# Query weights' low part moved to VectorE, both gates in one product, and GpSimd's subtractions cut into pieces

## The reference

```python
h = rms_norm(x, norm1_g) * (1.0 + scale1) + shift1
proj = h @ w_in
x_m, o_pre, i_fw, f_fw, i_bw, f_bw, a_q, a_k, a_v = split(proj)
y = concatenate([mlstm(x_m, o_pre, i_fw, f_fw, ...), dilated_attention(a_q, a_k, a_v, ...)])
x = x + gate1 * (y @ w_out)
x = x + gate2 * expert_choice_ffn(...)          # 16 experts
# second block, two layers on 16 meta tokens + 512
for l in range(2):
    parts = split(h @ w_in_2[l])
    mix = concatenate([retention(...), multiscale_pool(...), forgetting_attention(...)])
    h = layer_norm(ALPHA * h + mix @ w_out_2[l])
    h = layer_norm(ALPHA * h + (silu(h @ w1[l]) * (h @ w3[l])) @ w2[l])
```

## Time and profile before

| | us |
|---|---|
| median of 3 runs | 2998.18 (2996.76 to 3000.45) |
| profiled execution, its own time | 3000.69 |
| its span in the trace | 2998.7 |
| TensorE busy | 2733.4 |
| VectorE busy | 976.3 |
| GpSimd busy | 201.6 |

### The profile page before, as it was taken

One profiled execution on the slowest core, in us unless ns is written; L12 is line 12 of the kernel. 1 busy time (PEld: TensorE's weight loads), 2 busy tenths in 40 slices (PEclk: granted clock), 3 DMA queues, 4 the chain that ended last, 5 costly groups with the idle time before them and its releaser, 6 DMA issues.

```text
span 2998.7 us, 36825 instructions
## 1 busy us (share of the span) xinstructions
PE 2733.4 (91%) x15764; PEld 1949.3 (65%) x15764; DVE 976.3 (33%) x1582; ACT 683.6 (23%) x1169; POOL 201.6 (7%) x149
## 2 busy tenths in 40 slices
PE   6989676999999999999899889999999988999998
PEld 3756455444444444444387848999999775788886
DVE  4545544011111112111353344323324244433323
ACT  3214432001011001100232242222222224222222
POOL 2303010000000000000100500000000050000000
PEclk9999787899999999999999969999999997999998
DMA  7271013799999999999701201223231120132321
GB/s 257 91 259 66 1 31 142 304 420 425 427 427 424 428 428 426 426 426 428 292 30 57 64 1 57 85 82 109 76 97 48 57 64 1 57 108 85 110 77 57
DMA packets 238575, 558.33 MB, mean 186 GB/s; under 512 B 29601, under 2 KB 191779, under 8 KB 213500
## 3 DMA queue, kind: packets, MB, share of 16 engines
q1 hardware_dynamic: 234160, 548.48, 47.7%
q0 software_dynamic: 1552, 5.70, 0.6%
q10 hardware_dynamic: 2748, 2.47, 0.2%
HBM read 552.39 MB, written 4.23 MB: 186 GB/s over the span
## 4 chain that ended last, share of the span: by engine, by line
PE 85%; DVE 9%; ACT 3%; issue 2%; DMA 1%; SPq 1%; DVEq 0%; POOL 0%; PEldq 0%; ACTq 0%; POOLq 0%
PE vpsum L2127 20%; PE vpsum L1991 15%; PE apsum L2127 11%; PE vpsum L2008 8%; PE apsum L1975 4%; PE apsum L2136 3%; PE apsum L2153 2%; PE vpsum L2153 2%; PE vpsum L1773 2%; PE vpsum L1764 1%; PE vpsum L2038 1%; PE vpsum L2268 1%; PE apsum L2038 1%; PE vpsum L1849 1%; PE apsum L2057 1%
## 5 line engine op out<-in xcount | busy, mean ns | idle before, releaser
L1991 PE MATMUL vpsum<-ring,arena 128*64 128x512 f32 x2048 | 449.4, 597 | 0.8 <-ACT arena L964 0.8
L2127 PE MATMUL vpsum<-work_r,wring_r 128*128 128x264 f32 (+1 forms) x2160 | 346.2, 322 | 3.4 <-DVE work_r L1625 3.4
L2127 PEld LDWEIGHTS vpsum<-work_r,wring_r 128*128 128x128 f32 x2160 | 312.2, 189 | 37.6 <-issue 6.0
L2127 PE MATMUL apsum<-stream_r,wring_r 128*128 128x264 f32 (+1 forms) x2208 | 336.2, 312 | 0.0
L1991 PEld LDWEIGHTS vpsum<-ring,arena 128*64 128x64 f32 x2048 | 144.9, 138 | 282.9 <-issue 282.7
L2127 PEld LDWEIGHTS apsum<-stream_r,wring_r 128*128 128x128 f32 x2208 | 308.3, 192 | 22.2 <-issue 1.2
L1529 DVE TENSOR_TENSOR wring_r<-wring,wring_r 128x2048 fp32r<-128x2048 f32 (+2 forms) x97 | 200.3, 2069 | 353.1 <-ACT wring_r L1017 352.9
L2127 PE MATMUL vpsum<-stream_r,wring_r 128*128 128x264 f32 (+1 forms) x1728 | 273.8, 318 | 10.5 <-DVE body L1612 10.5
L1017 ACT ACTIVATE wring_r<-wring 128x2048 fp32r<-128x2048 f32 (+3 forms) x100 | 172.6, 1728 | 469.6 <-DMA wring<-w_ffn 453.0
L2127 PEld LDWEIGHTS vpsum<-stream_r,wring_r 128*128 128x128 f32 x1728 | 247.1, 192 | 31.8 <-DVE body L1612 10.9
L2008 PE MATMUL vpsum<-ring,arena 128*64 128x512 f32 x1024 | 226.8, 595 | 11.0 <-ACT arena L978 11.0
(11 more groups left out here) (428 smaller groups left out, 3145.5 us busy)
## 6 DMA issues: line engine op xcount, KB each, us to landing
ring<-w_gate SPq DMA_DIRECT2D x64, 2048.0 KB, 16.8
ring<-w_up SPq DMA_DIRECT2D x64, 2048.0 KB, 10.1
ring<-w_down SPq DMA_DIRECT2D x64, 2048.0 KB, 13.6
wring<-w_ffn SPq DMA_DIRECT2D x88, 512.0 KB, 4.7
ring<-w_ada SPq DMA_DIRECT2D x12, 2048.0 KB, 13.9
wring<-w_ffn SPq DMA_DIRECT2D x32, 704.0 KB, 4.5
ring<-w_in SPq DMA_DIRECT2D x5, 2048.0 KB, 18.9
wring<-w_in SPq DMA_DIRECT2D x10, 1024.0 KB, 5.4
```

The lines of the kernel that those rows point to most:

```text
L1991: last = pe.matmul(banks[g][CAP * blk:CAP * blk + CAP, :], xin[:, 2 * r + c, :], w[:, at:at + 512], start=r + c == 0, stop=r + c == 4)
L2127: last = pe.matmul(dst, w_[:, c, col:col + P], x_.bitcast(FR), start=c == 0 and i == 0, stop=c == chunks - 1 and i == 2)
```

## The change

- Query weights: the low part is made by VectorE in two halves of 128x2048, after all eight h chunks and before all eight low parts. TensorE waits for the new semaphore `q_low`.
- Gates: `wgate` is 104 columns wide, with the input gates at 0 and the forget gates at 64. One product per chunk fills one bank. The input gates are read with their bias; the forget gates are copied down to partition 0 and get their bias in a second instruction. A stage `gates_even` without contents keeps the count of stages, and the readers of the gates wait for it. The gate readers stand behind the eight low parts.
- GpSimd: the low parts of K_W, V_W, XM_W and O_W are made in four pieces of 1024 columns each, the casts and subtractions of the six units of the second block in four pieces of 512. No wait separates the pieces of one tensor.

```diff
@@
-        wgate = share(768, KC * 80, "p (c k m) -> p c k m", c=KC, k=2)
+        wgate = share(768, KC * GATE_W, "p (c m) -> p c m", c=KC)
@@ def input_low(i):
-                pool.tensor_tensor(ring_r[:, k, :].bitcast(FR), ring[:, k, :], ring_r[:, HIGH_SLOT[i], :], ALU.subtract).then_inc(in_low, 1)
+                for j in range(4):
+                    words = slice(1024 * j, 1024 * j + 1024)
+                    pool.tensor_tensor(ring_r[:, k, words].bitcast(FR), ring[:, k, words], ring_r[:, HIGH_SLOT[i], words], ALU.subtract).then_inc(in_low, 1)
@@
-            for i in (Q_W, K_W, V_W):
+            for i in (K_W, V_W):
                 input_low(i)
@@ for n in range(OP_U + 1, OP_U + 4):
-                    pool.tensor_copy(unit_part(l, n, True).bitcast(FR), unit_part(l, n, False, wring)).then_inc(w_high, 1)
+                    pieces = [slice(512 * j, 512 * j + 512) for j in range(4)]
+                    for piece in pieces:
+                        cut = pool.tensor_copy(unit_part(l, n, True)[:, piece].bitcast(FR), unit_part(l, n, False, wring)[:, piece])
+                    cut.then_inc(w_high, 1)
                     pool.wait_ge(w_high, LU * l + n + 1)
-                    pool.tensor_tensor(unit_part(l, n, False).bitcast(FR), unit_part(l, n, False, wring), unit_part(l, n, True), ALU.subtract).then_inc(w_low, 1)
+                    for piece in pieces:
+                        cut = pool.tensor_tensor(unit_part(l, n, False)[:, piece].bitcast(FR), unit_part(l, n, False, wring)[:, piece], unit_part(l, n, True)[:, piece], ALU.subtract)
+                    cut.then_inc(w_low, 1)
@@ VectorE
                 dve.tensor_scalar(hT[:, c, :], hT[:, c, :], g1s[:, c:c + 1], mod[:, c:c + 1], ALU.mult, ALU.add).then_inc(h_done, 1)
-                if c >= 1:
-                    stream_low(c - 1)
+            at = SLOT_OF[f"in{Q_W}"]
+            dve.wait_ge(in_high, Q_W + 1)
+            for k in range(2):
+                words = slice(2048 * k, 2048 * k + 2048)
+                dve.tensor_tensor(ring_r[:, at, words].bitcast(FR), ring[:, at, words], ring_r[:, HIGH_SLOT[Q_W], words], ALU.subtract).then_inc(q_low, 1)
+            for c in range(KC):
+                stream_low(c)
             dve.wait_ge(gate_in, 16 * 4)
-            for k in range(2):
-                dve.tensor_scalar(gates[0:40, k, :], take("gates", k)[0:40, :], bgate[:, k:k + 1], None, ALU.add).then_inc(v_freed, 1)
-            stream_low(KC - 1)
+            b = take("gates")
+            dve.tensor_scalar(gates[0:40, 0, :], b[0:40, :], bgate[:, 0:1], None, ALU.add).then_inc(gate_out, 1)
+            dve.tensor_copy(gates[0:40, 1, :], b[GATE_AT[1]:GATE_AT[1] + 40, :]).then_inc(gate_out, 1)
+            dve.wait_ge(gate_out, 2)
+            dve.tensor_scalar(gates[0:40, 1, :], gates[0:40, 1, :], bgate[:, 1:2], None, ALU.add).then_inc(v_freed, 1)
+            dve.wait_ge(v_freed, V.count("gates"))
+            take("gates_even")
+            dve.nop().then_inc(v_freed, 1)
@@ TensorE
-                for k in range(2):
-                    last = pe.matmul(banks[k][0:40, :], wgate[:, c, k, :], hT[:, c, :], start=c == 0, stop=c == KC - 1)
-                    if c == KC - 1 and k == 0:
-                        last.then_inc(v_filled, 1)
-                last.then_inc(h_used, 1)
+                pe.matmul(b[0:GATE_W, :], wgate[:, c, :], hT[:, c, :], start=c == 0, stop=c == KC - 1).then_inc(h_used, 1)
```

More of the change, by code:

```diff
@@ L22 @@
 MH, MD = 4, 128
+GATE_AT, GATE_W = (0, 64), 104
 AH, AD = 8, 64
@@ L238, in program @@
         MOD_ROW_AT = {1 + 4 * k: 8 + k for k in range(4)}
-        V = Plan([("xT", KC), ("colsA", 1)] + first_mods() + [("gates", 2), ("aqT", 4), ("akT", 4), ("colsA2", 1), ("colsB", 1), ("bvec", 3),
+        V = Plan([("xT", KC), ("colsA", 1)] + first_mods() + [("gates", 1), ("gates_even", 1), ("aqT", 4), ("akT", 4), ("colsA2", 1), ("colsB", 1), ("bvec", 3),
                   ("xm", MH)] + mod_stages(4, 8) + [("gcol", 2)] + list(attention_stages())
@@ L263, in program @@
         h_high, h_low1, in_high, in_low = sem("h_high"), sem("h_low1"), sem("in_high"), sem("in_low")
-        h_used, qk_scaled, h_normed, wgate_in, wgate_done, h2_scaled = sem("h_used"), sem("qk_scaled"), sem("h_normed"), sem("wgate_in"), sem("wgate_done"), sem("h2_scaled")
+        h_used, qk_scaled, h_normed, wgate_in, wgate_done, gate_out, q_low, h2_scaled = sem("h_used"), sem("qk_scaled"), sem("h_normed"), sem("wgate_in"), sem("wgate_done"), sem("gate_out"), sem("q_low"), sem("h2_scaled")
         wgate_rows = arena[:, 24336:24336 + KC * 16].rearrange("p (c n) -> p c n", c=KC)
@@ L645, in _ @@
                     for d in range(2):
-                        pool.tensor_copy(wgate[:, :, k, 32 * q + 4 * d:32 * q + 4 * d + 4], wgate_rows[:, :, 8 * d + 4 * k:8 * d + 4 * k + 4]).then_inc(wgate_done, 1)
+                        at = GATE_AT[k] + 32 * q + 4 * d
+                        pool.tensor_copy(wgate[:, :, at:at + 4], wgate_rows[:, :, 8 * d + 4 * k:8 * d + 4 * k + 4]).then_inc(wgate_done, 1)
             def input_low(i):
@@ L834, in _ @@
             input_high(K_W)
-            act.wait_ge(v_freed, V.count("gates"))
+            act.wait_ge(v_freed, V.count("gates_even"))
             tmp = gates[0:40, 2, :]
@@ L1777, in inputs @@
             def inputs(i):
-                pe.wait_ge(in_low, i + 1)
+                if i == Q_W:
+                    pe.wait_ge(q_low, 2)
+                else:
+                    pe.wait_ge(in_low, 4 * i)
                 return chunks(ring_r[:, HIGH_SLOT[i], :]), chunks(ring_r[:, SLOT_OF[f"in{i}"], :])
@@ L1788, in _ @@
             pe.wait_ge(wgate_done, 8)
-            banks = [vclaim("gates", k) for k in range(2)]
+            b = vclaim("gates")
             for c in range(KC):
                 pe.wait_ge(h_done, c + 1)
-                for k in range(2):
-                    last = pe.matmul(banks[k][0:40, :], wgate[:, c, k, :], hT[:, c, :], start=c == 0, stop=c == KC - 1)
-                    if c == KC - 1 and k == 0:
-                        last.then_inc(v_filled, 1)
-                last.then_inc(h_used, 1)
+                pe.matmul(b[0:GATE_W, :], wgate[:, c, :], hT[:, c, :], start=c == 0, stop=c == KC - 1).then_inc(h_used, 1)
             pe.wait_ge(h_used, KC)
+            pe.nop().then_inc(v_filled, 1)
+            vclaim("gates_even")
             pe.nop().then_inc(v_filled, 1)
```

## The result

The change makes the kernel faster: 2975.65 us (median of 4 runs, 2974.12 to 2980.6) against 2997.68 of the kernel before on the same chip, a ratio of 0.993 (95% interval 0.991 to 0.994). A second time, with 6 runs: 2976.7 (2969.3 to 2981.6) against 2998.66, 0.992 (0.991 to 0.994). The forecast was 2974.7, range 2966 to 2986. The profiled execution took 2977.05, its span 2975.3, which is 23.4 less than before; the sum said 23.5. The sum came out, but two of its terms did not: place 2 gave less than forecast, the layers more. A second profiled execution of the changed kernel took 2969.43 us, with a span 31.0 us shorter than before, so one pair of traces does not settle the sum.

A forecast was written before the change was run, and what follows sets the result against it. TensorE, busy 91%, was taken to bound the kernel, so gains come only where it waits for VectorE or GpSimd. 8.2 + 7.5 + 7.8 = 23.5 us less than 2998.18 gives 2974.7 us, range 2966 to 2986.

The forecast's parts named there:

- the sum: Whole kernel: gains of 8.2 at the start, 7.5 at the output gate and 7.8 in the layers, together 23.5 us.
- place 2: Output gate stage: shorter GpSimd pieces let VectorE's late chain finish earlier, so TensorE waits less and runs warm; 7.5 us.
- Place 1: Kernel start: query products begin at 56.1 instead of 66.13, less 1.8 us for a cold clock; 8.2 us gained.
- Rival (a): Start and layers: the fast TENSOR_SCALAR does not contend with GpSimd; sum 27.4, time 2970.8 us; chance 0.22.
- Rival (b): Start: GpSimd's pieces meet VectorE's low parts, two more pieces, 4.5 us; time 2979.2 us; chance 0.13.
- Rival (d): Query and key products: clock stays at 1.2 GHz after the new 8 us wait; 3016.5 us, slower; chance 0.03.
- Together the chain is some 5.2 us earlier: Output gate stage: VectorE's chain ends 5.2 us earlier, shrinking TensorE's wait of 5.85 us to 0.7.
- The scan's turn comes after one piece: Output gate stage, first scan: it waits 2.25 us instead of 9; only 0.4 to 0.9 us won until 131 us.
- it also runs warm: Output gate stage: the row product and block behind take 1.85 + 5.68 instead of 3.57 + 6.14; another 2.2 us.
- Rival (c): All cut places: a train of pieces without waits keeps its turn against VectorE; 2997.6 us; chance 0.09.
- No scan over 4 us: Sign expected in the new profile: no VectorE scan would take longer than 4 us.
- Place 3: Both layers: five mix_low subtractions near 7.7 instead of 12.59 us, less 1.0 charged for later GpSimd pieces; 7.8 us together.

The follow-up runs named there:

- the kernel in which the scan was first: Changed kernel with GpSimd waiting between the four xm weight pieces, the first held back until VectorE's step just ahead of its scan: 2976.72 us, one run.
- the layers alone: Kernel before with only the layers' GpSimd casts and subtractions cut into pieces of 512: 2990.92 us, 0.997, 7.7 us less.

## Why the prediction was right, and where not

**What bounds.** Right: all that moved did so at the three places. The expert stage gives nothing back: from TensorE's last transposition ahead of it to the first of the second block it lasts 969.19 us (508.37 to 1477.56), before 969.41 (521.57 to 1490.98).

**Place 1, 8.2 us: measured 8.17.** The start at 56.1 was 56.19, the cold clock 1.8 us. It rested on the fast TENSOR_SCALAR being blocked, read from its rate alone. Rival (a) falls: 2.31 and 8.62 us beside GpSimd, 0.48 alone. By the rule of the Trainium skill (SBUF — State Buffer, Who interferes with whom) such an instruction can contend with GpSimd; the trace agrees. Rival (b), pieces among the low parts, did not happen: 4.90 us for eight. Rival (d) neither: full speed at 60 us. (Its break-even is 50.6 us of half speed by its own terms, twice the 25.3, and not 47.)

**Place 2, 7.5 us: measured 4.5 (2.9 in the second trace).** The step that failed is "Together the chain is some 5.2 us earlier". Beyond the earlier start it was 3.1 us earlier (fifth reciprocal at 156.91 before and 145.61 after, 11.3 us, less 8.2), and both of its parts were off. "The scan's turn comes after one piece": it came after the train, 10.62 us, so that the chain was 0.4 us later at the second scan (7.7 us earlier with a start 8.2 earlier) instead of 0.4 to 0.9 us ahead. "The SCALAR_TENSOR_TENSOR waits about 0.2 us instead of 6.0, the next about 1.2": they waited 1.1 us each. So TensorE's wait was 2.71 us, not 0.7, and behind it the row product stayed cold, not warm.

The scan alone does not explain the shortfall. In the kernel without the layer pieces and in the one with pauses it took 3.32 and 3.41 us, as predicted, and TensorE still waited 2.71 us: the SCALAR_TENSOR_TENSOR then came up just as a piece started and waited 2.2 us for all of it. In the kernel in which the scan was first and took 1.21 us, the first reciprocal was another 0.33 us earlier (124.35 for 124.68), the same instruction was over in 0.75 us, only the next waited, 1.1 us, and TensorE waited 0.45. Where the chain stands against the four pieces of the output gate weights thus decides over 2.2 us, and the prediction had put it in one place without a margin.

The price behind the wait is half shown. In all four kernels in which the scan is not held for the train and a load decides, the row product is at its load, but only the one with the xm pieces ahead of the Hankel load runs warm and gains 7.6 us. In the other three it takes 2.41 to 3.04 us and the stage 94.62 to 94.89, 5.6 to 5.9 us gained: "it also runs warm", 2.2 us of the sum, does not follow from the load.

Rival (c), "the train of pieces keeps its turn", had been given 0.09 for the whole kernel; it is true at this one instruction, and false everywhere else. "No scan over 4 us" and a wait of under 1.5 us at L1735 were the signs that the prediction named, and both came out against it. The Trainium skill (SBUF — State Buffer, Who interferes with whom) says that the order of issue decides who blocks. By the recorded starts that would let the scan through each time: in the kernel in which pauses stand between the pieces it was so (1.21 us), in five traces without pauses it was not. The recorded starts lie within 0.1 us of each other, and whether they are the order of issue no run shows.

**Place 3, 2 x 3.9 us: measured 9.2 and 2.1.** The turns are right: 7.50 us against 7.7. What was charged for the later end of GpSimd's work was too much: L1661 was met, but its first five instructions took 2.6 us more in sum than before (0.31, 0.47, 0.77, 1.13 and 1.28 us for 0.22, 0.22, 0.30, 0.30 and 0.36), and the idle time before each unit took up all but some 0.5 us. 5.1 us less 0.5 is 4.6, close to the difference of 92.04 and 87.50, each kernel at its better clock. What makes 9.2 and 2.1 of it is the granted clock: before had its 96.7 in layer 0 and its 92.0 in layer 1, after 87.5 and 90.0. No term of the sum had this. The split into 4.6 us of work and the rest of clock is argued from these values; the layers alone, measured as a kernel, gave 7.7 us for both, which is the term as forecast.

**The sum, 23.5: measured 22.0 by medians, 23.4 by the two traces.** That it came out so closely is luck: in this pair of traces place 2 was 3.0 us too high and the layers together 3.5 too low, by the split above more of it clock than work. The changed kernel itself ran between 2969.3 and 2981.6 us, so 2 us are no proof of a term; each stands on its own stage.

## What to carry to other kernels

Where GpSimd and VectorE share SBUF, the length of one GpSimd instruction is what a VectorE instruction waits for: cut GpSimd's work where VectorE is on the path, and ask first whether the waiting instruction can be put ahead of it, which costs no time (moving three gate instructions gave 7.5 us at the start, cutting alone 1.4). Cutting sets a maximum for each wait, but which instruction meets a piece, and when, can still move the result by the length of a piece. A stage is best priced from its own start to its own end, since the clock of another stage can hide or double the result; and from more than one trace, since the output gate stage of one kernel took 96.00 and 97.58 us. After each gain look for what is late next: here it was a load, in one case one that the same edit had delayed.

## What was not expected of the hardware

A TENSOR_TENSOR_SCAN of 8x512 (1.21 us alone) that is recorded 0.01 to 0.09 us ahead of a train of four GpSimd subtractions without pauses is held for the whole train (10.5 to 10.6 us, 5 of 5 traces), and the train's first piece is not slowed (2.4 us). With GpSimd 0.20 us ahead of the same scan it waits for one piece (3.32 us), and other VectorE instructions take turns with the train, 2.5 to 2.8 us each. And TensorE's granted clock in a stretch full of short waits differs from one execution to another: the same code took 96.7 or 92.0 us.
